# Weighting the experts' rows by their gates at readout, and letting the DMA add both rows onto the residual in the last stage

## The reference, cut to what matters

```python
    hg = lax.ragged_dot(xs, w_gate, sizes)
    hu = lax.ragged_dot(xs, w_up, sizes)
    ye = lax.ragged_dot(jax.nn.silu(hg) * hu, w_down, sizes)
    ye = ye * gates.reshape(-1)[order][:, None].astype(ye.dtype)
    y = jax.ops.segment_sum(ye, tok, num_segments=T)
...
        x = layer_norm(DEEPNORM_ALPHA * x + (1.0 + g2[:, None]) * y, ln_g[i, 1], ln_b[i, 1])
```

## Time and profile before

| | us |
|---|---|
| median of the 3 runs (lowest 3112.1, highest 3117.61) | 3112.36 |
| the profiled execution | 3118.38 |
| its span, first to last instruction | 3116.6 |
| last stage in it, from 2987.45 to the end | 129.2 |

### The profile page before, as it was taken

The page is one execution under the profiler, slowest core; times in us unless marked ns, Lnnn a source line. Parts: engine busy times, 40 slices in busy tenths (PEclk is TensorE's granted clock), DMA queues, the critical chain, the costliest instruction groups (busy, mean ns, idle before and its releaser), DMA issues. The chain is left out here.

```text
span 3116.6 us, 41489 instructions
## 1 busy us (share of the span) xinstructions
PE 2785.0 (89%) x14798; PEld 2330.0 (75%) x14798; DVE 2224.6 (71%) x2623; ACT 1298.8 (42%) x1624; POOL 1514.7 (49%) x817
## 2 busy tenths in 40 slices
PE   7599999999999999999938999967999999999910
PEld 2288888888888888888816888856888888888810
DVE  2567778777787778787742333456888888888868
ACT  1233333333333333333331111115777767776722
POOL 0023343333433343433401222216899999999965
PEclk9799999999999999999958999978999999999955
DMA  6754544445444544445142323228887878678667
GB/s 233 301 199 163 206 169 160 163 172 203 170 165 164 205 169 160 163 172 190 54 155 90 115 102 107 95 95 297 329 319 267 296 264 322 238 267 292 244 232 242
DMA packets 249588, 619.01 MB, mean 199 GB/s; under 512 B 15346, under 2 KB 97906, under 8 KB 240756
## 3 DMA queue, kind: packets, MB, share of 16 engines
q1 hardware_dynamic: 225556, 530.27, 47.4%
q0 software_dynamic: 11520, 41.95, 4.0%
q10 hardware_dynamic: 12384, 45.09, 3.6%
HBM read 609.65 MB, written 99.88 MB: 228 GB/s over the span
## 5 line engine op out<-in xcount | busy, mean ns | idle before, releaser
L1515 DVE TENSOR_TENSOR piece_lo<-piece_raw,piece_hi 128x2048 fp32r<-128x2048 f32 x187 | 563.2, 3031 | 102.4 <-ACT piece_hi L1620 102.3
L1620 ACT CAST piece_hi<-piece_raw 128x2048 fp32r<-128x2048 f32 x280 | 526.2, 1909 | 205.7 <-DVE ye L1680 156.0
L1515 POOL TENSOR_TENSOR piece_lo<-piece_raw,piece_hi 128x2048 fp32r<-128x2048 f32 x93 | 566.0, 6086 | 26.1 <-ACT piece_hi L1620 24.0
L572 PE MATMUL pj<-hm,w_hi 128*128 128x512 f32 x2048 | 533.4, 406 | 25.3 <-DMA hm<-hm_parts 22.0
L841 DVE SCALAR_TENSOR_TENSOR cv<-ub,par,cv 128x512 f32<-128x512 f32 x384 | 385.4, 1004 | 170.9 <-ACT cv L719 161.8
L572 PEld LDWEIGHTS pj<-hm,w_hi 128*128 128x128 f32 x2048 | 379.1, 190 | 101.3 <-DMA hm<-hm_parts 23.6
L536 POOL TENSOR_TENSOR xw<-xw,t 128x512 f32<-128x512 f32 x64 | 96.8, 1512 | 474.6 <-DVE t L907 474.6
L587 PE MATMUL pz<-wz_hi,hm 128*128 128x256 f32 x2048 | 294.7, 289 | 0.7
L587 PEld LDWEIGHTS pz<-wz_hi,hm 128*128 128x128 f32 x2048 | 264.4, 191 | 6.5 <-DVE wz_lo L819 3.5
L572 PE MATMUL pj<-hm,w_lo 128*128 128x512 f32 x1024 | 254.8, 391 | 0.0
L572 PEld LDWEIGHTS pj<-hm,w_lo 128*128 128x128 f32 x1024 | 192.2, 188 | 43.1
(11 more groups left out here) (292 smaller groups left out, 5881.7 us busy)
## 6 DMA issues: line engine op xcount, KB each, us to landing
hm<-hm_parts SPq DMA_DIRECT2D x32, 4096.0 KB, 13.3
piece_raw<-in_w_gate SPq DMA_DIRECT2D x94, 1024.0 KB
piece_raw<-in_w_up SPq DMA_DIRECT2D x94, 1024.0 KB
piece_raw<-in_w_down SPq DMA_DIRECT2D x92, 1024.0 KB
decay<-acum_rows SPq DMA_DIRECT2D x32, 1024.0 KB, 4.7
w_raw<-in_w_in SPq DMA_DIRECT2D x48, 512.0 KB, 7.6
expert_out<-ye ACTq DMA_DIRECT2D x46, 512.0 KB, 6.6
hm_parts<-hl SPq DMA_DIRECT2D x4, 4096.0 KB, 16.0
```

The costliest lines, as they stand in the source:

```text
L572: mm = nc.tensor.matmul(pj[m % 2][:], wp[m][:, kk, :], hm[b][:, hp, kk, :], start=q == 0, stop=q == 3 * KK - 1)
L1515: v.tensor_tensor(lo[q][:], raw[q][:], hi[q][:].bitcast(F32), ALU.subtract).then_inc(lo_done[q], 1)
L1620: nc.scalar.copy(hi[q][:], raw[q][:]).then_inc(hi_done[q], 1)
```

## The change

In the experts' stage the gates get the same treatment as the token numbers: DVE keeps the one-hot tile matrices as `weights`, multiplies them by the gates, PE multiplies `lanes` by `weights` into the PSUM bank `up` (32 more matmuls of 66 columns), and DVE copies the result to `slot_gates`, one gate per slot. The readout of the down product then multiplies by the slot's gate and by g2 in one instruction. The first product waits for that copy (`gates_ready`), since it shares the bank. `lane` and `weights0` lie in the memory of the last piece's high and low part, so ACT casts that piece only after the gates' matmuls. All six pieces of tile 0 are loaded at once, DVE's first two low parts stand ahead of `ids`, and SP starts on tile 1's weights after the first gather has landed, not after `ids`.

In the last stage SP loads the residual straight into one of eight buffers `r`. POOL issues for each tile a gather of the first expert row with addition onto `r`, and after that has landed a gather of the second one with addition. The first is issued four tiles ahead (A), the second two tiles ahead (B). DVE reads the statistics from `r` and needs two more instructions: o = (r - mean) * weight, and o = o * rstd + bias. ACT has nothing to do.

```diff
@@ experts
+        weights.append(sb("weights1", [P, TT, NTAB]))
+        gates = sb("slot_gates", [P, NTAB])
...
-            load(0, range(GU))
+            load(0, range(PIECES))
             sp.dma_start(g2[:], k.g2d[0].partition_broadcast(P)).then_inc(g2_in, 16)
-            sp.wait_ge(ids_ready, 1)
+            sp.wait_ge(x_in[0], 16)
             loop(sp, step)
...
+                if not in_loop(t, 1):
+
+                    pe.wait_ge(gates_ready, 1)
                 for q in range(GU):
...
+            for c in range(2):
+                pe.wait_ge(weights_done, c + 1)
+                for t in range(TT):
+                    mm = nc.tensor.matmul(up[:, 0:NTAB], lanes[c][t // 8][:, t % 8, :], weights[c][:, t, :],
+                                          start=c == 0 and t == 0, stop=c == 1 and t == TT - 1)
+            mm.then_inc(gates_mm, 1)
             turn(0, 0)
...
-                nc.vector.tensor_tensor(ye[b][:, n * 512:(n + 1) * 512], yp[n][:], g2[:, n * 512:(n + 1) * 512],
-                                        ALU.mult).then_inc(ye_done, 1)
+                nc.vector.scalar_tensor_tensor(out=ye[b][:, n * 512:(n + 1) * 512], in0=yp[n][:],
+                                               scalar=gates[:, bass.ds(t, 1)], in1=g2[:, n * 512:(n + 1) * 512],
+                                               op0=ALU.mult, op1=ALU.mult).then_inc(ye_done, 1)
...
+            dve.wait_ge(marks_done, 2)
+            for c, gate in enumerate((k.gate_a, k.gate_b)):
+                v.tensor_tensor(weights[c][:], weights[c][:], over(gate[:], TT, NTAB), ALU.mult
+                                ).then_inc(weights_done, 1)
+            dve.wait_ge(gates_mm, 1)
+            v.tensor_copy(gates[:], up[:, 0:NTAB]).then_inc(gates_ready, 1)
@@ output
-        R = 4
+        R, A, B = 8, 4, 2
...
+            def add(i, slots, needed, arrived):
+
+                s, turn = i % R, 16 * (i // R + 1)
+                pool.wait_ge(needed[s], turn)
                 pool.sem_inc(k.passed, 1)
...
+                nc.gpsimd.indirect_dma_start(out=r[s][:], out_offset=None, in_=k.ysd[:],
+                                             in_offset=bass.IndirectOffsetOnAxis(ap=slots[:, i:i + 1], axis=0),
+                                             compute_op=ALU.add).then_inc(arrived[s], 16)
+
+            for i in range(-A, TT):
+                if i + A < TT:
+                    add(i + A, k.slot_a, xa_in, ya_in)
+                if 0 <= i + B < TT:
+                    add(i + B, k.slot_b, ya_in, yb_in)
+                if i >= 0:
+                    pool.wait_ge(ve_done, i + 1)
+                    if i >= 2:
+                        pool.wait_ge(o_done, i - 1)
+                    nc.gpsimd.tensor_tensor(rstd[i % 2][:], ve[:], k.negh[:, 0:1], ALU.pow).then_inc(rstd_done, 1)
...
+                nc.vector.scalar_tensor_tensor(out=o[i % 2][:], in0=o[i % 2][:], scalar=rstd[i % 2][:], in1=lnb[:],
+                                               op0=ALU.mult, op1=ALU.add).then_inc(o_done, 1)
...
+                nc.vector.scalar_tensor_tensor(out=o[i % 2][:], in0=r[s][:], scalar=mv[:, 0:1], in1=lng[:],
+                                               op0=ALU.subtract, op1=ALU.mult).then_inc(og_done, 1)
```

More of the change, by code:

```diff
@@ L1428, in experts @@
         raw = [sb(f"piece_raw{q}", [P, 4, 512]) for q in range(PIECES)]
-        hi = [sb(f"piece_hi{q}", [P, 4, 512], F32R) for q in range(PIECES)]
-        lo = [sb(f"piece_lo{q}", [P, 4, 512], F32R) for q in range(PIECES)]
+        hi = [sb(f"piece_hi{q}", [P, 4, 512], F32R) for q in range(PIECES - 1)]
+        lo = [sb(f"piece_lo{q}", [P, 4, 512], F32R) for q in range(PIECES - 1)]
+        with ExitStack() as early:
+            lane = [k.makers(early)[0](f"lane{n}", [P, 8, P]) for n in range(2)]
+            weights = [k.makers(early)[0]("weights0", [P, TT, NTAB])]
+        hi.append(sb(f"piece_hi{PIECES - 1}", [P, 4, 512], F32R))
+        lo.append(sb(f"piece_lo{PIECES - 1}", [P, 4, 512], F32R))
         ix = [sb(f"ix{b}", [P, 1], I32) for b in range(2)]
@@ L1445, in experts @@
         cand, pm = th[:], a[:]
-        lanes = [[t[:].rearrange("p (t q) -> p t q", q=P) for t in pair] for pair in (xg, ye)]
-        marks = [raw[q][:].rearrange("p a b -> p (a b)")[:, 0:TT * NTAB].rearrange("p (t n) -> p t n", n=NTAB)
-                 for q in (4, 5)]
+        lanes = [[t[:] for t in lane], [t[:].rearrange("p (t q) -> p t q", q=P) for t in ye]]
+        marks = [sb(f"marks{c}", [P, TT, NTAB]) for c in range(2)]
+        weights.append(sb("weights1", [P, TT, NTAB]))
+        gates = sb("slot_gates", [P, NTAB])
         xp = first
@@ L1501, in step @@
                 load(t + 1, range(GU))
-                load(t, range(GU, PIECES))
-            load(0, range(GU))
+                if in_loop(t, 1):
+                    load(t, range(GU, PIECES))
+            load(0, range(PIECES))
             sp.dma_start(g2[:], k.g2d[0].partition_broadcast(P)).then_inc(g2_in, 16)
-            sp.wait_ge(ids_ready, 1)
+            sp.wait_ge(x_in[0], 16)
             loop(sp, step)
@@ L1650, in step @@
                                      ).then_inc(ht_hi_done, 1)
-                high_part(GU + 1, t)
                 if in_loop(t, 1):
+                    high_part(GU + 1, t)
                     store(t - 1, 1 - b)
-            for q in range(GU):
+            for q in range(PIECES - 1):
                 high_part(q, 0)
             xt_high(0)
+            act.wait_ge(gates_mm, 1)
+            high_part(PIECES - 1, 0)
             last = loop(act, step)
@@ L1792, in output @@
         sb, ps, sem = k.makers(ctx)
-        R = 4
+        R, A, B = 8, 4, 2
         lng, lnb = (sb(n, [P, D]) for n in "lng2 lnb2".split())
[L1795 to L1805, removed]
+        r = [sb(f"r2_{s}", [P, D]) for s in range(R)]
+        o = [sb(f"o_{b}", [P, D]) for b in range(2)]
+        bst, mv, ve = sb("bst2", [P, 2, 6]), sb("mv2", [P, 2]), sb("ve2", [P, 1])
+        rstd = [sb(f"rstd2{b}", [P, 1]) for b in range(2)]
+        row_in, bn_done, mv_done, ve_done, rstd_done, og_done, o_done = (
+            sem(n) for n in "row_in bn2 mv2s ve2s rstd2s og_done o_done".split())
         ya_in, yb_in, xa_in = ([sem(f"{n}{s}") for s in range(R)] for n in ("ya_in", "yb_in", "xa_in"))
@@ L1808, in output, with load @@
         block = ctx.enter_context(nc.Block())
[L1810 to L1817, removed]
         @block.sync
         def _(sp):
[L1821 to L1840, removed]
+            def load(i):
+                if i >= R:
+                    sp.wait_ge(og_done, i - R + 1)
+                sp.dma_start(r[i % R][:], k.xad[i]).then_inc(xa_in[i % R], 16)
+            for i in range(R):
+                load(i)
+                if i == 2:
+                    for row, src in ((lng, k.d["ln_g"][1]), (lnb, k.d["ln_b"][1])):
+                        sp.dma_start(row[:], src.partition_broadcast(P)).then_inc(row_in, 16)
+            for i in range(TT):
+                if i + R < TT:
+                    load(i + R)
+                sp.wait_ge(o_done, i + 1)
+                sp.dma_start(out[i * P:(i + 1) * P, :], o[i % 2][:]).then_inc(stored[i % 2], 16)
             for b in range(2):
@@ L1860, in step @@
[L1860 to L1871, removed]
@@ L1935, in _, with finish @@
-            loop(dve, step, 1)
+            def finish(i):
+                dve.wait_ge(rstd_done, i + 1)
+                dve.wait_ge(og_done, i + 1)
+                nc.vector.scalar_tensor_tensor(out=o[i % 2][:], in0=o[i % 2][:], scalar=rstd[i % 2][:], in1=lnb[:],
+                                               op0=ALU.mult, op1=ALU.add).then_inc(o_done, 1)
+            dve.wait_ge(row_in, 32)
+            for i in range(TT):
+                s = i % R
+                dve.wait_ge(yb_in[s], 16 * (i // R + 1))
+                if i:
+                    dve.wait_ge(mv_done, i)
+                for n in range(2):
+                    nc.vector.bn_stats(bst[:, n, :], r[s][:, n * 512:(n + 1) * 512]).then_inc(bn_done, 1)
+                dve.wait_ge(bn_done, 2 * (i + 1))
+                if i:
+                    dve.wait_ge(og_done, i)
+                nc.vector.bn_aggr(mv[:], bst[:].rearrange("p a b -> p (a b)")).then_inc(mv_done, 1)
+                dve.wait_ge(mv_done, i + 1)
+                if i:
+                    dve.wait_ge(rstd_done, i)
+                nc.vector.tensor_scalar(ve[:], mv[:, 1:2], EPS, None, ALU.add).then_inc(ve_done, 1)
+                if i:
+                    finish(i - 1)
+                if i >= 2:
+                    dve.wait_ge(stored[i % 2], 16 * (i // 2))
+                nc.vector.scalar_tensor_tensor(out=o[i % 2][:], in0=r[s][:], scalar=mv[:, 0:1], in1=lng[:],
+                                               op0=ALU.subtract, op1=ALU.mult).then_inc(og_done, 1)
@@ L1938 @@
+            finish(TT - 1)
 class Kit:
```

84 lines of the change are left out of this document (14 added, 70 removed).

## The result

| | before | after |
|---|---|---|
| median, us (8 runs each on one chip) | 3115.45 | 3126.72 |
| lowest to highest, us | 3112.1 to 3120.12 | 3122.79 to 3130.84 |
| span of the profiled execution, us | 3116.6 | 3129.0 |

The ratio is 1.0033 with an interval of [1.0023, 1.0042]: slower by 7 to 13 us, where 11.5 us of gain were forecast. The median of before comes from more runs here than the 3112.36 that the forecast started from. The change of +11.3 us is close to rival A's +12.9.

The account below looks back on a forecast made before the run. DVE set the last stage's pace, with the DMA as new bound; PE bound the experts' loop. Last stage -14.6 us and experts' head +3.1 gave -11.5: 3106.9 profiled, median 3100.9, range 3084 to 3132 (the forecast's own 3092 to 3107).

Parts of the forecast that it names:

- rival A: Last stage: the add's second read is paid, 2.5 us an add, period 7.05, whole +12.9 (3125 us); chance 0.31.
- the price p of an add: Last stage: DMA engine time per gather with addition, taken as a plain gather's 1.70 us, between 1.25 and 3.4.
- 2p + 2.03: Last stage: period per tile in us from two adds plus one store and half a load, no less than 4.7; forecast 5.4.
- The share of 0.91 at 303 GB/s: Last stage before the change: DMA busy time, read as partly waiting a second read could fill, since 418 GB/s was seen.
- The head: Last stage, start to first `ve`: residual 4, two adds 9.1 each, statistics 1.9; 24.1 us against 17.5.
- DVE's relief: Last stage: DVE keeps statistics and two three-operand instructions, 4.5 to 4.6 us a tile.
- the tail: Last stage after the last `ve`: three DVE instructions, then store and program end; 9.1 us for 11.5.
- the gates' matmuls at half clock all the way: Experts' stage head: 32 added matmuls take 14.1 us at half clock; 7.05 if at full clock.
- the late transposes: Experts' stage head: transposes wait for the gates' matmuls until 2126.0, so the first product comes 3.1 us later.
- nothing in the loop: Experts' loop: readouts cost at most 0.05 us more each, covered by DVE's 2.3 us idle a tile; no change.
- C: Last stage: adds at the lower end, 1.25 us each, POOL's 4.7 us as period, stage 103.7, time 3090; chance 0.10.
- its bound at p = 2.1: Last stage: add price in us at which stage plus the experts' +3.1 equals the old 129.2, deciding against the change.

Follow-up runs that it names:

- e1: The changed kernel with both last-stage gathers plain, overwriting the buffer, so residual and first row are missing from the sum: 3098.18 us, ratio 0.9939.
- e4: The changed kernel with one add a tile: the second row is gathered plainly into its own buffer and DVE adds it; 3116.49 us, 0.9998 against before.
- e5: The changed kernel with plain gathers (sum left out) plus two extra 512 KB loads a tile from ACT's queue into unread buffers: 3124.18 us.
- e7: Before's experts' stage with a new last stage: plain gathers, PE sums residual and gate-weighted rows in PSUM, DVE as in the changed kernel; 3093.41 us, 0.9926.

## Why the prediction was wrong

**The failed step is the price p of an add.** I took 1.70 us, a plain gather's row, with 1.25 and 3.4 as ends. By the queue's share it was 2.63, by the periods 2u = 2.52, which is the value that the text worked out for both reads at 418 GB/s and laid aside. The period with loads and stores is then 7.6, with stores alone 6.3; 15 of them made 99.7 us, where the forecast had 81.4. That is +18.3 of the stage's +23.5 over the forecast. The bound itself was named rightly: the DMA took over from DVE. What was mis-sized is p in 2p + 2.03.

**Two readings led there.** The share of 0.91 at 303 GB/s was read as waiting that a second read could fill. That room was not enough: with the adds the engines ran full at 274 to 276 GB/s of payload, and 405 x 4/6 = 270 is what counting an add twice gives. And 1.70 was taken as a gather's own price. In e1, with full engines, it was (5.16 - 2u) / 2 = 1.32. So the queue's share over its transfers, taken at a share of 0.91, gave more than the transfer needs; what the difference consists of, no run here shows. The row was too dear for the gather and too cheap for the add.

The rule cited in the prediction, from the Trainium skill ("Collectives: The Full Stack", section "The bandwidth ceiling: the fold count and why AG ≠ RS ≠ AR"), says that an add inside the DMA reads two sources through the same ring and so gets half a copy's rate. The traces agree in the size: 2.52 us for 1.26. The runs show the doubled price; that it is the second read that causes it is the page's statement, and no run here separates it from another doubling inside the DMA.

**The head** was forecast as a chain of three links, and the trace has these three in that order, each longer than forecast. The first add was issued 4.6 us after the start (forecast 4), the first second add 11.7 us after that and the statistics 11.2 us later again (forecast 9.1 each): 29.0 for 24.1, +4.9. Plain gathers in the same chain (e1) gave 2990.93 to 3014.78, 23.9 us, so the extra length comes from the additions. But the chain is not what keeps the head long: in e4 the second row waits for no add, and the head is 29.2 us. The DMA engines were full in both heads (a share of 1.04 from 2993 to 3019 in after and from 2992 to 3018 in e4), with eight residuals, two broadcast rows and eight adds or gathers asked for in that time. That speaks for the engines as the limit here too, which a forecast that added up single landings left out. How much of the head another order of the first transfers would give back, no run shows.

**A's number is in part luck.** A had the price right (2.5) and the change of the whole nearly so (+12.9 for +11.3), but from 105.8 us of periods, where 99.7 were measured, and a head of 24.1, where 29.0 were. The two misses cancel. The periods came out shorter because of the first three (4.9 to 7.1 us), part of whose adds ran in the head already, and the last (4.03), where DVE alone was left.

**Right.** DVE's relief (its bare period, the last one, was 4.03 us for the 4.5 expected), the tail (9.4 for 9.1), the gates' matmuls at half clock all the way, the late transposes (first product 18.2 us after `fresh` for 18.8, the stage +2.3 for +3.1), and nothing in the loop. With plain gathers at 1.32, near C's condition, the stage was 106.8 (e1; C: 103.7, with POOL's 4.7 as the period, where the DMA gave 5.16).

**The chances.** The text had its bound at p = 2.1 between 1.25 and 3.4 and named the row that it stood on as a choice. What should have weighed more: the change takes nothing off the DMA and it gives the DMA work that a compute engine did, while the DMA's share was 0.91 already. With p open and only that said, A deserved more than 0.31.

## What to carry to other kernels

Before moving arithmetic into a transfer, count the transfers a tile in the stage, an add as two, and multiply by the time of one at the highest steady rate that the trace shows; if the sum is above what the compute engine needs now, the move loses. If it is below, count the stage's head too: in e4 the 15 periods took 12.3 us less than before and the head 11.7 us more. A queue's share divided by its transfers overstated the price here (1.70 for 1.3) when the engines weren't full: take it from the bytes at the best rate. When a wait moves from one transfer to another as buffers are added and the period stays, the resource is full, and only fewer transfers, or another engine, help.

## What the runs showed of the hardware

- An indirect gather of 128 rows of 4 KB with addition into SBUF took the 16 DMA engines 2.5 to 2.6 us, without it about 1.3; at a share of 1.06 the payload was 274 to 276 GB/s, without additions 405 at 1.02 (e1) and 416 at 1.03 (e5).
- Its issue on POOL took 1.59 us (median of 16; 986 ns for the plain one in e1), and with full engines it landed 14 us after issue where the plain one took 8.
- On PE the 32-bit matmuls of 66 columns ran at half clock (1.2 GHz) in both blocks of after: the granted clock was 0.50 from 2095 to 2111 (PE busy 14.5 of 16 us) and from 2113 to 2127 (13.9 of 14). In e7's last stage PE came out of a pause of 20.2 us into matmuls of 512 columns; the granted clock was 0.60 on average from 2996 to 3000 and 1.00 (2.4 GHz) from 3000 to 3020.
